# The opening of a two-layer hybrid diffusion block: first modulation by column chunks, squares added on the vector engine

## The chip, the cores and the metric

The kernel runs on one core of one Trainium2 chip. It is written engine by engine: TensorE (PE) for matrix products, VectorE (DVE), ScalarE (ACT) and GpSimd (POOL) for the rest, SyncE (SP) for issuing transfers. Each engine works through its own list in order, and semaphores tie the lists together. The metric is device time of one execution in microseconds (us), the median over runs; all arithmetic is float32.

## The reference

Two layers over 256 latent tokens and 256 context tokens of width 1024. What matters here is the start of a layer:

```
ml = (silu(c) @ w_mod[l] + b_mod[l])            # 6 x 1024 numbers for the latent tokens
mc = (silu(c_ctx) @ w_mod[l] + b_mod[l])        # the same for the context tokens
hl = rms_norm(xl, norm1_g) * (1 + ml[1]) + ml[0]
hc = rms_norm(xc, norm1_g) * (1 + mc[1]) + mc[0]
pl, pc = hl @ w_in[l], hc @ w_in[l]             # combined input projection, then three token mixers
```

One of the mixers (Hyena) needs filter spectra that depend on weights alone: a small two-layer sine network (`fw1`, `fw2`, angle and sine each time), a third product `w3s` times a decay (the filters), its absolute sum, and a discrete Fourier transform of the sum and the difference of its two halves. Each layer has two such filters, o = 0 and o = 1. After the mixers come an output projection, a second modulated norm and a mixture of 16 experts.

## The kernel before

Activations stand feature-major: `xT` is 128 partitions x 8 blocks x 512 tokens. Before a projection the modulated input is split into a leading and a trailing part, `h_hi` and `h_lo` (block k of 8), and each weight half (128 columns) into `w_hi` and `w_lo`; a tile of the projection is 8 k-steps of three matmuls (lines 1020 to 1022). The first two tiles of layer 0 are run abreast, k-step by k-step (`proj_steps`), so that they can begin when block 0 of the input is ready; tiles 2, 3, ... follow whole.

All weights of the opening pass through a ring of 3 slots of 1 MB. The Python list `order` says what goes through it and in which order; SP issues the loads in that order, each behind a wait for its slot. In the kernel before the list starts with the 8 pieces of the first modulation (`("mod", 0, k)`: 128 rows of `w_mod`, columns 0 to 2047), then the chunks of `w_in` (`("in", 0, i)`), two weight halves each. The slot of a `w_in` chunk is free once GpSimd has written `w_lo` of both its halves (`trail`), which follows ScalarE's `w_hi` (`lead_in`).

The opening of layer 0, by engine:

- TensorE: the sums of squares for the norm as 8 matmuls with a matrix of ones (`norm_sum`), the 8 modulation pieces (`mod`, each adds its 128 rows to the same bank), the filter products (`filters(0, 0)`), `spectra_a`, transposes of the modulation row (`mod_columns`), `spectra_b`, `filters(0, 1)`, then the two tiles abreast. Tile 3 waits until DVE has finished tiles 0 and 1 (`pe.wait_ge(j_d[l], g - 1)`).
- ScalarE: squares of `xT`, two sines, the rough inverse root of the norm, copies of spectra and of the modulation row, `lead_in`, then the latent half's scale and shift and `h_hi`, block by block.
- VectorE: angles of the sines, the norm's mean and refinement (`norm_dve_root`), `taps` (filter products times decay, sum, difference, absolute values), the modulation's bias and gain, then for each block the norm's scale (line 2241), the context half's scale and shift (line 2246) and `h_lo` (line 2254), three blocks behind; after that `taps(0, 1)` and the short convolution of each tile (lines 2366 and 2368).

## Time and profile before

| | us |
|---|---|
| median of 3 runs (lowest, highest) | 1566.31 (1566.29, 1572.91) |
| the profiled execution's own time | 1569.26 |
| its span in the trace | 1567.6 |
| TensorE busy in the span | 1471.8 (94%) |
| first k-step of the two tiles abreast starts | 54.68 |

The profiled execution took 2.95 us more than the median, and 1.66 us of its time lie outside the span. In the rows below a time is counted from the start of the span. A group of matmuls in a timeline counts each float32 matmul as two records.

### The profile page before, as it was taken

The page shows a single profiled execution, that of the slowest core. Times are in us where ns is not written, and L with a number is a line of the kernel's source. Part 1 is how long each engine was busy: PE and PEld are TensorE (multiplying, and loading weights), DVE is VectorE, ACT ScalarE, POOL GpSimd, SP SyncE. Part 2 cuts the span into 40 slices and gives each one's busy share as a digit, 9 for nine tenths or more (in the row PEclk, how much of TensorE's full clock was granted, in tenths as well). Part 3 has the DMA queues.
Part 4 walks back from the last instruction along what each step waited for, and adds up shares of the span by engine and source line. Part 5 has one row for each costly group of instructions (what it writes and reads, how often), then busy time and mean ns, then how long its engine had stood idle before and what let it go on. Part 6 is the DMA issues. An engine that isn't in the chain of part 4 may idle for free.

```text
span 1567.6 us, 20695 instructions
## 1 busy us (share of the span) xinstructions
PE 1471.8 (94%) x8212; PEld 1086.9 (69%) x8212; DVE 877.5 (56%) x1266; ACT 632.7 (40%) x853; POOL 406.1 (26%) x367
## 2 busy tenths in 40 slices
PE   6999999899999997899999999999988997999997
PEld 2588788657777784678888874697868995445444
DVE  4725556774222347799999967664783566111112
ACT  2532222264222335477787755442264443010102
POOL 0446334201333440111101013473414661000000
PEclk9999999999999998899999999998999999999997
DMA  8423211376456573799999983252304766899993
GB/s 330 147 81 107 81 55 59 133 279 223 160 191 205 190 277 126 267 370 403 406 409 405 397 314 122 65 185 81 102 22 152 259 233 276 329 420 420 422 421 133
DMA packets 116898, 362.78 MB, mean 231 GB/s; under 512 B 7774, under 2 KB 73632, under 8 KB 85952
## 3 DMA queue, kind: packets, MB, share of 16 engines
q1 hardware_dynamic: 109296, 334.62, 56.5%
q0 software_dynamic: 7504, 26.81, 4.6%
q8 instruction: 67, 1.10, 0.3%
q14 instruction: 31, 0.25, 0.0%
HBM read 349.86 MB, written 11.53 MB: 231 GB/s over the span
## 4 chain that ended last, share of the span: by engine, by line
PE 49%; DVE 10%; issue 2%; ACT 1%; DMA 0%; POOL 0%; DVEq 0%; PEldq 0%; ACTq 0%
PE bank L1020 9%; PE bank L1021 9%; PE bank L1022 9%; PE bank L1540 7%; PE bank L1579 4%; PE bank L1493 2%; PE bank L1479 1%; PE bank L1549 1%; PE bank L1504 1%; PE bank L1097 1%; PE bank L1231 1%; PE bank L1606 1%; PE bank L1011 1%; PE bank L1607 1%; DVE mix L2403 0%
## 5 line engine op out<-in xcount | busy, mean ns | idle before, releaser
L833 POOL TENSOR_TENSOR w_lo<-ring,w_hi 128x256 fp32r<-128x256 f32 (+1 forms) x300 | 347.8, 1188 | 515.0 <-ACT w_hi L1864 515.0
L1020 PE MATMUL bank<-h_hi,w_hi 128*128 128x512 f32 (+1 forms) x768 | 272.1, 354 | 8.8 <-POOL w_lo L833 3.4
L1021 PE MATMUL bank<-h_hi,w_lo 128*128 128x512 f32 (+1 forms) x768 | 263.1, 343 | 0.0
L1022 PE MATMUL bank<-h_lo,w_hi 128*128 128x512 f32 (+1 forms) x768 | 263.0, 342 | 0.0
L1020 PEld LDWEIGHTS bank<-h_hi,w_hi 128*128 128x128 f32 x768 | 146.5, 191 | 41.1 <-issue 16.5
L1021 PEld LDWEIGHTS bank<-h_hi,w_lo 128*128 128x128 f32 x768 | 146.6, 191 | 16.8 <-issue 1.4
L1022 PEld LDWEIGHTS bank<-h_lo,w_hi 128*128 128x128 f32 x768 | 146.5, 191 | 16.8
L1020 PE MATMUL bank<-w_hi,h_hi 128*128 128x512 f32 (+1 forms) x384 | 141.8, 369 | 6.7 <-DVE h_lo L2785 3.1
L1864 ACT ACTIVATE w_hi<-ring 128x1024 fp32r<-128x1024 f32 x120 | 125.4, 1052 | 40.5 <-PE bank L1020 31.4
L1021 PE MATMUL bank<-w_hi,h_lo 128*128 128x512 f32 (+1 forms) x384 | 138.1, 360 | 0.0
L1022 PE MATMUL bank<-w_lo,h_hi 128*128 128x512 f32 (+1 forms) x384 | 137.7, 359 | 0.0
L2561 DVE SCALAR_TENSOR_TENSOR mix<-mix,bank 128x512 f32<-128x512 f32 (+1 forms) x48 | 26.5, 553 | 168.5 <-PE bank L1022 116.7
L1020 PEld LDWEIGHTS bank<-w_hi,h_hi 128*128 128x128 f32 x384 | 74.1, 193 | 17.7 <-issue 3.7
L2043 ACT ACTIVATE mix<-bank 128x256 f32<-128x256 f32 (+1 forms) x39 | 18.8, 481 | 165.9 <-PE bank L1022 164.2
L2617 DVE TENSOR_TENSOR w_lo<-ring,w_hi 128x2048 fp32r<-128x2048 f32 x32 | 73.3, 2292 | 17.4 <-ACT w_hi L2073 17.4
L1022 PEld LDWEIGHTS bank<-w_lo,h_hi 128*128 128x128 f32 x384 | 74.0, 193 | 10.8
L1021 PEld LDWEIGHTS bank<-w_hi,h_lo 128*128 128x128 f32 x384 | 74.1, 193 | 10.4 <-issue 0.5
L2617 DVE TENSOR_TENSOR w_lo<-mix,w_hi 128x2048 fp32r<-128x2048 f32 x32 | 73.1, 2284 | 2.3 <-ACT w_hi L2073 2.3
L2073 ACT ACTIVATE w_hi<-mix 128x2048 fp32r<-128x2048 f32 x32 | 61.4, 1918 | 22.1 <-PE bank L1022 22.1
L994 POOL TENSOR_SCALAR mix<-xT,fin_g 128x256 f32<-128x256 f32 x4 | 3.6, 919 | 253.8 <-DVE xT L2917 253.8
L2073 ACT ACTIVATE w_hi<-ring 128x2048 fp32r<-128x2048 f32 x32 | 61.2, 1915 | 19.3 <-PE bank L1022 19.3
L1540 PE MATMUL bank<-operands_plain,mix 128*64 128x512 f32 x248 | 63.9, 594 | 0.0
(367 smaller groups left out, 2865.6 us busy)
## 6 DMA issues: line engine op xcount, KB each, us to landing
ring<-in_w_in SPq DMA_DIRECT2D x52, 1024.0 KB, 5.0
mix<-in_w_gate_e SPq DMA_DIRECT2D x40, 1024.0 KB, 7.8
ring<-in_w_up_e SPq DMA_DIRECT2D x38, 1024.0 KB, 8.1
mix<-in_w_down_e SPq DMA_DIRECT2D x25, 1024.0 KB, 8.3
ring<-in_w_mod SPq DMA_DIRECT2D x24, 1024.0 KB, 6.0
ring<-in_w_down_e SPq DMA_DIRECT2D x23, 1024.0 KB, 7.5
mix<-in_w_mod SPq DMA_DIRECT2D x19, 1024.0 KB, 4.9
operands_plain<-in_w_up_e SPq DMA_DIRECT2D x16, 1024.0 KB, 12.3
```

Source lines behind the costliest of these rows:

```text
L833: last = pool.tensor_tensor(w_lo[:, slot, k:k + n], rview(raw, 8)[:, k:k + n, x * P:(x + 1) * P], w_hi[:, slot, k:k + n].bitcast(F32), ALU ...
L1020: first = mm(dst, stat[0], mov[0], start=start, stop=False)
L1021: mm(dst, stat[1], mov[0], start=False, stop=False)
L1022: return first, mm(dst, stat[0], mov[1], start=False, stop=stop)
L1493: last = mm(bank[i][:, k * P:(k + 1) * P], htok[:, j, (4 * i + k) * P:(4 * i + k + 1) * P], hot_rows[l][e % 2][:, j, :], start=j == 0, sto ...
L1540: last = mm(dst[x * M:(x + 1) * M, :], heT[:, 0, 4 * h + k, x * M:(x + 1) * M], raw(l, c)[:, k * FF:(k + 1) * FF], start=h + k == 0, stop= ...
L1579: last = mm(y_bank[o][x * M:(x + 1) * M, :], hidT[:, 0, 2 * h + k, x * M:(x + 1) * M], raw(l, c)[:, k * D + o * 512:k * D + (o + 1) * 512] ...
L1864: A(w_hi[:, slot], rview(raw, 8)[:, :, x * P:(x + 1) * P], ACT.Copy).then_inc(w_h, 1)
L2043: A(gate_t[:, m % 2, 0:T], gate_v, ACT.Tanh, scale=0.5).then_inc(g_t[l], 1)
L2073: A(xhi[c % XH], raw(0, c), ACT.Copy).then_inc(x_wh, 1)
L2561: last = V.scalar_tensor_tensor(gated, gate_t[:, m % 2, 0:T], 1.0, bank[2 + m % 2][:, 0:T], ALU.add, ALU.mult)
L2617: V.tensor_tensor(xlo[c % XH], raw(0, c), xhi[c % XH].bitcast(F32), ALU.subtract).then_inc(x_wd, 1)
```

## The change

- `w_mod` of the first modulation is laid out on the host in 8 column chunks (`w_mod_first`): piece p holds, for all 1024 input rows, the 128 shift columns and the 128 gain columns of feature block p. A piece therefore gives the finished modulation of block p alone (`first_piece`: 8 matmuls of 32 rows x 256 columns; four strips of the bank hold partial sums). ScalarE copies the strips (`first_rows`), TensorE adds the strips and turns them into columns with `strip_sum` (`first_columns`), and DVE adds the bias and makes the gain (`first_take`) for blocks 0 to 3 together, 4, 5, 6, and 7. ScalarE scales block k when its part is there (`first_scale`).
- The first `w_in` chunk moves in the ring order to behind the first four modulation pieces.
- `w3s` and `decay` are loaded ahead of the modulation pieces.
- The 8 squares are added on DVE (`squares_added`, 7 additions) and one matmul sums the result, in place of 8 matmuls.
- DVE puts the norm's mean between the two parts of `taps(0, 0)`, and its refinement before the absolute values.
- `spectra_a`, `spectra_b` and the first k-steps of the tiles abreast are cut into steps and set between the pieces; `filters(0, 1)` moves behind the two tiles abreast.

```diff
+IN_AFTER = 4
+MORE = 7
+TAKES = [(0, 4), (4, 5), (5, 6), (6, 7), (7, 8)]
+TAKES_AT = [0, 2, 4, 5, 7]
...
         order = [("mod", 0, k) for k in range(DK)]
+        order.insert(IN_AFTER, ("in", 0, 0))
...
+            def first_piece(p):
+
+                at = at_of[("mod", 0, p)]
+                pe.wait_ge(ring_full[at % RS], full_at(at))
+                if p:
+                    pe.wait_ge(m_ev[0], p)
+                for j in range(2):
+                    for c in range(4):
+                        k = 2 * c + j
+                        last = mm(bank[5][32 * c:32 * c + 32, 0:256], csil[:, k, :], ring[:, at % RS, k * 256:(k + 1) * 256],
+                                  start=j == 0, stop=j == 1)
+                last.then_inc(ring_used, 1)
+
+            def first_columns(p):
+
+                pe.wait_ge(m_ev[0], p + 1)
+                if p >= TAKES[0][1]:
+                    pe.wait_ge(m_tk[0], p)
+                for c in range(2):
+                    last = mm(bank[6][:, 4 * p + 2 * c:4 * p + 2 * c + 2], piece_rows[p % 2][:, c * P:(c + 1) * P], strip_sum,
+                              start=True, stop=True)
+                last.then_inc(m_co[0], 1)
 
             filter_in(0, 0)
+            filter_in(0, 1)
             pe.wait_ge(s_ld, 16 * 2)
-            for k in range(4):
-                norm_sum(0, NT, k)
             pe.wait_ge(s_c, 2)
-            mod(0, 0, 0)
-            filter_in(0, 1)
-            for k in range(4, DK):
-                norm_sum(0, NT, k)
-            mods_and_filters(0, range(1, DK))
-            filters(0, 1)
+            filters(0, 0)
+            first_piece(0)
+            norm_sum_added(0, NT)
+            first_piece(1)
...
-                for _ in zip(*(proj_steps(g) for g in range(ABREAST[l]))):
+                abreast_steps = zip(*(proj_steps(g) for g in range(ABREAST[l])))
+                if l == 0:
+                    a_steps, b_steps = spectra_a_steps(0, 0), spectra_b_steps(0, 0)
+                    first_columns(0)
+                    first_piece(2)
+                    first_columns(1)
+                    next(a_steps)
+                    first_piece(3)
+                    first_columns(2)
+                    next(a_steps)
+                    first_piece(4)
+                    first_columns(3)
+                    next(b_steps)
+                    first_piece(5)
+                    first_columns(4)
+                    next(b_steps)
+                    next(abreast_steps)
+                    first_piece(6)
+                    first_columns(5)
+                    next(b_steps)
+                    next(abreast_steps)
+                    first_piece(7)
+                    first_columns(6)
+                    next(abreast_steps)
+                    first_columns(7)
+                for _ in abreast_steps:
                     pass
+                if l == 0:
+                    filters(0, 1)
...
+                    first_rows(1)
+                    first_rows(2)
+                    first_rows(3)
+                    lead_in(0)
+                    lead_in(1)
+                    spectrum_a(0, 0)
+                    first_rows(4)
+                    first_scale(0)
...
+            def first_take(lo, hi):
+
+                n = hi - lo
+                dve.wait_ge(m_co[0], hi)
...
+                        if inst == 0 and k in TAKES_AT:
+                            first_take(*TAKES[TAKES_AT.index(k)])
...
             angle(0, 0)
             angle(0, 1)
-            norm_dve_root(0, NT)
-            taps(0, 0)
-            mod_first(0)
+            dve.wait_ge(s_ld, 16 * 2)
+            V.tensor_reduce(strip_sum, ident.rearrange("p (c x) -> p x c", c=4)[:, 0:2], AX.X, ALU.add)
+            for k in range(1, DK):
+                squares_added(0, NT, k)
+            taps(0, 0, norm_dve_mean)
+            norm_dve_rest(0, NT)
+            taps_size(0, 0)
```

How it moves the lists, at three places. The first is SP's list at its start (`in_w_mod` and `in_w_mod_first` are modulation pieces, `in_hy_w` is `w3s`, `in_w_in` a chunk of the projection). Before:

```order
L711 DMA xT<-in_x_cols 128x4096
L779 DMA ring<-in_w_mod 128x2048 x3
L715 DMA mix<-in_hy_w 128x1024
L716 DMA mix<-in_decay 128x1024
L718 DMA dft_f<-in_dft_f 128x1024
L719 DMA nyq<-in_nyq 128x2
L779 DMA ring<-in_w_mod 128x2048 x5
L779 DMA ring<-in_w_in 128x8x256
```

and of the change:

```order
L725 DMA xT<-in_x_cols 128x4096
L726 DMA mix<-in_hy_w 128x1024
L727 DMA mix<-in_decay 128x1024
L798 DMA ring<-in_w_mod_first 128x2048 x3
L735 DMA dft_f<-in_dft_f 128x1024
L736 DMA nyq<-in_nyq 128x2
L798 DMA ring<-in_w_mod_first 128x2048
L798 DMA ring<-in_w_in 128x8x256
L798 DMA ring<-in_w_mod_first 128x2048 x4
L744 DMA dft_z<-in_dft_z 128x512
```

The projection chunk now stands ahead of four of the modulation pieces, and the filter weights ahead of all.

The second place is TensorE's list from the filter products to the end of the first half of `spectra_b` (L1070 and L1092 filters, L1047 and L1151 modulation pieces, L1079 and L1108 `spectra_a`, L1161 `first_columns`). Before:

```order
L1070 MATMUL bank<-mix 128x512 x4
L1047 MATMUL bank<-ring,csil 32x512 x8
L1079 MATMUL bank<-mix,dft_f 128x512 x4
L1082 MATMUL bank<-mix,nyq 1x512 x2
L1047 MATMUL bank<-ring,csil 32x512 x8
L1029 MATMUL bank<-square,mix 128x128 x4
L1092 MATMUL bank<-square,mix 128x1 x8
```

and of the change:

```order
L1161 MATMUL bank<-small,mix 128x2 x2
L1108 MATMUL bank<-mix,dft_f 128x512 x2
L1113 MATMUL bank<-mix,nyq 1x512 x2
L1151 MATMUL bank<-ring,csil 32x256 x8
L1161 MATMUL bank<-small,mix 128x2 x2
L1129 MATMUL bank<-square,mix 128x1 x8
L1151 MATMUL bank<-ring,csil 32x256 x8
```

Each piece is now followed by its own small column products, and by a part of the spectra.

The third place is TensorE's list where the two tiles abreast end. Before, the second filter (L1070) stands ahead of them:

```order
L1092 MATMUL bank<-square,mix 128x1 x8
L1097 MATMUL bank<-mix,dft_f 128x512 x4
L1070 MATMUL bank<-mix 128x512 x4
L1020 MATMUL bank<-h_hi,w_hi 128x512
L1021 MATMUL bank<-h_hi,w_lo 128x512
L1022 MATMUL bank<-h_lo,w_hi 128x512
```

and of the change, where it (L1092) stands between the last k-step of tiles 0 and 1 and the first of tile 2:

```order
L1039 MATMUL bank<-h_hi,w_hi 128x512
L1040 MATMUL bank<-h_hi,w_lo 128x512
L1041 MATMUL bank<-h_lo,w_hi 128x512
L1092 MATMUL bank<-mix 128x512 x4
L1039 MATMUL bank<-h_hi,w_hi 128x512
```

`filters(0, 1)` has moved from ahead of 16 k-steps to behind them.

## Rows read from the trace of the kernel before

**Rows 1.** The page's first line.

```profile
span 1567.6 us, 20695 instructions
```

**Rows 2.** Timeline of TensorE, 50 to 78 us: start, duration, line, operation.

```profile
52.45 1.99 PE L1070 MATMUL bank<-mix 64*128 64x512 f32 x8 [1.72 <-ACT mix L1838]
54.68 0.47 PE L1020 MATMUL bank<-h_hi,w_hi 128*128 128x512 f32 x1 [0.24 <-DVE h_lo L2254]
...
71.70 3.60 PE L1079 MATMUL bank<-mix,dft_f 128*128 128x512 f32 x8
75.23 1.88 PE L1082 MATMUL bank<-mix,nyq 128*1 128x512 f32 x4
77.03 0.50 PE L1020 MATMUL bank<-h_hi,w_hi 128*128 128x512 f32 x1
```

**Rows 3.** Timeline of VectorE, second filter and first convolutions.

```profile
63.59 2.48 DVE L2310 TENSOR_TENSOR mix<-bank,mix 128x512 f32<-128x512 f32 x4
...
75.15 0.75 DVE L2368 SCALAR_TENSOR_TENSOR mix<-bank,par,mix 128x510 f32<-128x510 f32 x1
```

**Rows 4.** Timeline of TensorE, 12 to 52 us.

```profile
12.50 6.68 PE L1004 MATMUL bank<-mix,square 128*128 128x512 f32 x8 [6.78 <-ACT mix L1772]
19.10 1.07 PE L1047 MATMUL bank<-ring,csil 128*32 128x512 f32 x8
...
30.43 1.06 PE L1047 MATMUL bank<-ring,csil 128*32 128x512 f32 x8 [1.25 <-DMA ring<-in_w_mod]
32.93 1.94 PE L1047 MATMUL bank<-ring,csil 128*32 128x512 f32 x8 [1.43 <-DMA ring<-in_w_mod]
...
45.34 1.84 PE L1092 MATMUL bank<-square,mix 128*128 128x1 f32 x16
47.05 3.68 PE L1097 MATMUL bank<-mix,dft_f 128*128 128x512 f32 x8
```

**Rows 5.** Busy time by stretch: engines, granted clock, DMA share, GB/s.

```profile
core 0: us, PE busy (x) PEld busy (x) DVE busy (x) ACT busy (x) POOL busy (x), PEclk, DMA share, GB/s
...
30.00:32.00 2.00, 1.06 (x8) 0.16 (x8) 1.84 (x4) 0.00 (x0) 0.00 (x0) 1.00 1.01 426
32.00:34.00 2.00, 1.07 (x8) 0.20 (x8) 1.97 (x3) 0.00 (x0) 0.00 (x0) 0.55 1.02 430
...
38.00:40.00 2.00, 2.00 (x5) 0.72 (x3) 0.00 (x0) 0.00 (x0) 0.00 (x0) 0.74 0.85 274
```

**Rows 6.** Timeline of ScalarE, 11 to 47 us.

```profile
11.72 1.15 ACT L1772 ACTIVATE mix<-xT 128x512 f32<-128x512 f32 x2 [6.93 <-DMA xT<-in_x_cols]
...
44.69 2.00 ACT L1864 ACTIVATE w_hi<-ring 128x1024 fp32r<-128x1024 f32 x2
```

**Rows 7.** Timeline of VectorE, 20 to 56 us.

```profile
20.84 0.54 DVE L2293 TENSOR_SCALAR mix<-bank,par 128x256 f32<-128x256 f32 x1 [12.19 <-PE bank L1058]
...
23.45 0.29 DVE L2301 TENSOR_SCALAR mix<-mix 128x256 f32<-128x256 f32 x1
...
29.29 2.48 DVE L2310 TENSOR_TENSOR mix<-bank,mix 128x512 f32<-128x512 f32 x4 [0.99 <-PE bank L1070]
...
36.11 1.23 DVE L2321 TENSOR_TENSOR mix<-mix 128x1024 f32<-128x1024 f32 x1
...
45.77 0.80 DVE L2274 SCALAR_TENSOR_TENSOR gs<-mods,par 128x8 f32<-128x8 f32 x2
46.49 1.81 DVE L2241 TENSOR_TENSOR mix<-xT,mix 128x512 f32<-128x512 f32 x2
...
53.84 0.69 DVE L2254 TENSOR_TENSOR h_lo<-mix,h_hi 128x512 fp32r<-128x512 f32 x1 [1.07 <-ACT h_hi L1805]
...
55.05 0.41 DVE L2246 TENSOR_SCALAR mix<-mix,gs,mods 128x256 f32<-128x256 f32 x1
```

**Rows 8.** Timeline of GpSimd, the trailing halves of the weights.

```profile
45.82 7.53 POOL L833 TENSOR_TENSOR w_lo<-ring,w_hi 128x256 fp32r<-128x256 f32 x8 [45.25 <-ACT w_hi L1864]
62.72 2.85 POOL L833 TENSOR_TENSOR w_lo<-ring,w_hi 128x256 fp32r<-128x256 f32 x4 [9.37 <-ACT w_hi L1864]
```

**Rows 9.** SP's queue, modulation pieces 4 to 6 being issued.

```profile
25.61 2.05 SPq L779 DMA_DIRECT2D ring<-in_w_mod x3
```

More of the change, by code:

```diff
@@ L231, in build @@
         mod_next = area(16384, 2048)
+        piece_rows = [area(21504 + 256 * i, 256) for i in range(2)]
+        strip_sum = small[:, 12:14]
         mrows = [[area(o, 512) for o in (21504, 17536, 19968)], [area(o, 512) for o in (19968, 19968)]]
@@ L1065, in filters @@
                     pe.wait_ge(f_a[l], 6 * l + 2)
-                    pe.wait_ge(s_lds, transforms_to(l))
+                    if l:
+                        pe.wait_ge(s_lds, transforms_to(l))
+                    else:
+                        pe.wait_ge(s_ldl[0], 32)
                 for j in range(2):
@@ L1083, in spectra_a, with spectra_b_steps @@
                 last.then_inc(f_p[l], 1)
+                yield
             def spectra_b(l, o):
+                for _ in spectra_b_steps(l, o):
+                    pass
+            def spectra_b_steps(l, o):
                 pe.wait_ge(f_d[l], 10 * l + 5 + 4 * o)
@@ L1788, in norm_act_scale @@
                     if w == 0:
[L1789 to L1791 removed]
+                        scale_h(inst, k)
                         if k:
@@ L1884, in _ @@
                     act.wait_ge(j_pe[l], g + 1)
+                    if l == 0 and g == 0:
+                        act.wait_ge(f_p[l], 6)
                     if g in (4, 8):
@@ L2301, in angle, with taps @@
                 V.tensor_scalar(x0, x1, 3.1415925, -3.1415925, ALU.min, ALU.max).then_inc(f_d[l], 1)
-            def taps(l, o):
+            def taps(l, o, between=None):
                 r, pm = fraw[l][o], fpm[l][o]
                 dve.wait_ge(f_p[l], 8 * l + 3 + 3 * o)
-                dve.wait_ge(s_lds, transforms_to(l))
+                if l:
+                    dve.wait_ge(s_lds, transforms_to(l))
+                else:
+                    dve.wait_ge(s_ldl[0], 32)
                 for i in range(2):
@@ L2313, in taps @@
                 dve.wait_ge(dve_c, chain[0])
+                if between is not None:
+                    between(2 * l, NT)
                 link(V.memset(r[0:1, 1, 0, :], 0.0))
@@ L2317, in taps, with taps_size @@
                 V.tensor_tensor(pm[:, 1], r[:, 0], r[:, 1], ALU.subtract).then_inc(f_d[l], 1)
+                if between is None:
+                    taps_size(l, o)
+            def taps_size(l, o):
+                r = fraw[l][o]
                 dve.wait_ge(f_d[l], 10 * l + 4 + 4 * o)
```

144 lines of the change are left out of this document (92 added, 52 removed).

## The prediction

> **What bounds the kernel now.** I read the page first for the span, 1567.6 us [rows 1], then the timelines of the five engines over the first 110 us, since nothing else is rebuilt. TensorE has three stages there. Up to 54.68 it waits often: for `xT`, then for modulation pieces (idle 1.25 and 1.43 us ahead of two of them), then for a ScalarE copy, and at 54.68 for the first `h_lo` [rows 2, 4]. From there it runs without a gap: tiles 0, 1 and 2 are 72 matmuls from 54.68 to 71.70, that is 5.67 us a tile and 1.42 us for a k-step of two tiles abreast; then `spectra_a(0, 1)` (3.60 and 1.88), then tile 3 at 77.03 [rows 2]. So whatever the change does to the time is what it does to the start of tile 3, which I use as the mark: from 77.03 on both kernels have the same lists on each engine, and the loads behind it are released by engines that stand later in the same chain, so they move with it.
>
> One more reading matters. In the trace before, VectorE starts `taps(0, 1)` at 63.59, as soon as it is through with `h_lo`, because the products of `filters(0, 1)` have been ready since 54.44. It has done the convolutions of tiles 0 and 1 at 75.90 [rows 3]: 12.3 us of work. Tile 3 needs them. In the kernel before they are 1.1 us early, so the wait is not seen.
>
> **The change, step by step.** I write hops between engines as 0.1 us.
>
> *Up to VectorE's first block.* `xT` lands at 11.7 [rows 6]. The second filter layer's angle takes 2.9 (20.84 to 23.74 [rows 7]). Its matmul is now ahead of it: one of 128x512 took 1.67 (6.68 for four [rows 4]), this one has half the columns; with the sine of about 0.4 the angle runs 13.2 to 16.2. An addition of squares is one of the 0.69 operations [rows 7]; the first ends at 17.1, squares 2 and 3 (0.6 each [rows 6]) stand ahead of the second sine on ScalarE, so that ends at 18.8. The seven additions end near 22.4.
>
> *TensorE's clock here.* The four matmuls from 12.50 took 1.67 us each, while at full clock four of the same size took 3.60 [rows 2, 4]: the engine starts at the lower of its two levels (1.2 GHz), though no clock event shows it. The row for 32 to 34 us shows it granted 0.55 after two gaps around a single piece, and the piece from 32.93 took 1.94 in place of 1.06; it came back at 39, with the engine busy all the while [rows 4, 5]. In the changed kernel TensorE has nearly nothing to do before 18.8, so I take `filters(0, 0)` at the lower level: 2 x 1.99 less the tail, 3.8 [rows 2], to 22.6; piece 0 1.94, to 24.6; the norm's matmul 0.9 to 1.7 [rows 2, 4], to 25.8; piece 1 to 26.9.
>
> *VectorE.* Before, `taps(0, 0)` is 8.05 from 29.29 to 37.34 [rows 7]. Its first 2.5 are done at 25.2, the mean (0.7) at 26.5, then 5.6 for the rest and 2.1 for three refinements: 34.2. It starts block 0 there and not at 46.49 [rows 7]. That is 12.3 us earlier, and it is the most the change can hand on.
>
> *The ring.* Piece 1 frees the slot of the `w_in` chunk, issued at 27.0. A load into an idle queue was issued at 25.61 and used at 30.43, 4.8 us [rows 4, 9], so it lands at 31.9. ScalarE copies the rows of pieces 1 to 3 first; piece 3 stands behind half of `spectra_a` (1.8) and ends at 32.0. Then the two `w_hi` (2.0 [rows 6]), the first done at 33.4, and GpSimd's eight operations: 7.53 beside a busy VectorE, 2 x 2.85 = 5.7 with a less busy one [rows 8]. VectorE waits part of that time for its columns, so I take the middle, 6.6: done at 40.1. SP's next load, piece 6, waits for exactly this, and piece 7 and all tables stand behind it in SP's list. Piece 6 lands at 40.2 + 4.8 = 45.0, piece 7 one transfer later: 1 MB at 426 GB/s [rows 5] is 2.5, so 47.5.
>
> The Trainium skill (SBUF — State Buffer, "SBUF: two separate sides") states that VectorE and GpSimd share a port pair under an exclusive lock, taken by whichever starts first, when a VectorE operation has two SBUF inputs. By that, GpSimd would stretch to the 7.53 only while VectorE is working, and pieces 6 and 7 would come up to 0.9 us later or earlier than I take it; the trace agrees in kind, with 7.53 for eight operations beside VectorE's busiest stretch.
>
> *The tiles abreast.* Piece 4 follows the second half of `spectra_a` (2.8, with the two row products) and ends at 36.1, so blocks 0 to 3 have their modulation near 37. Piece 5 follows the sums of `spectra_b` (1.84 [rows 4]) and ends at 39.2, its columns at 39.5. VectorE must take block 4 before it reaches `h_lo` of block 0: take 0.6, context scale 0.4, norm scale 0.7, context scale 0.4, `h_lo` 0.7 [rows 7] put k-step 0 at 42.3 instead of 54.68. But VectorE's list puts the take of block 5 ahead of `h_lo` 1, of block 6 ahead of `h_lo` 2, of block 7 ahead of `h_lo` 4. After piece 6 (45.1 to 46.1, columns 0.3) come a take (about 0.6: one operation of 0.40 and a smaller one), the context scale (0.41) and `h_lo` (0.69) [rows 7]: k-step 1 at 48.2 to 49.6, piece 7 to 50.7, again 2.1 on the chain: k-step 2 at 52.8 to 54.3, k-step 3 at 54.6 to 56.1; a further 2.4 of VectorE's list (scale, take, context, `h_lo`) puts k-step 4 at 57.2, and the last ends at 62.9. Before, tiles 0 and 1 ended at 54.68 + 11.3 = 66.0. So of the 12.3 us, 3.1 are left here.
>
> *Behind them.* `filters(0, 1)`, 1.99 [rows 2], now comes here and ends at 64.9. From there TensorE needs tile 2 and `spectra_a`, 5.67 + 5.33 = 11.0, but VectorE needs 12.3 from the same moment, and tile 3 waits for VectorE: 64.9 + 0.1 + 12.3 = 77.3. That is 0.3 us later than before. The 1.1 us of slack are used, and the wait for the columns and the second filter's late start have eaten the rest.
>
> *The clock once more.* Between 40.2 and 45.1 TensorE has 1.4 us of work. The gaps that lost the clock before were shorter [rows 4, 5], so I expect the lower level at about 44. Piece 6 then costs 0.9 more, and the second half of `spectra_b` behind it (half of 3.68 [rows 4]) about 1.8 more, of which some is hidden behind the chain over VectorE. With recovery somewhere in there, this is 0.9 to 2.9; I take 1.7. The Trainium skill (TensorE: Matmul & The Clock Gate, "What's actually happening") says that the throttled state is the default and that activity releases it. That rule speaks against a list with a wait between every two pieces; by the rows the same comes out.
>
> Sum: +0.3 + 1.7 = +2.0 us. Against its own execution that is 1569.26 + 2.0 = 1571.3; that execution stood 2.95 above the median of 1566.31, so the median is forecast at 1568.3. Removed work (7 matmuls of the norm, the transposes) stands at nothing, since TensorE waits there anyway; if that cover were gone it would be 7 x 0.9 = 6 us.
>
> **Rivals.**
>
> 1. *The clock stays up, GpSimd runs free.* Pieces 6 and 7 come 0.9 earlier and no matmul is slow: 77.3 - 0.9 = 76.4, 0.6 us before 77.03, and a load latency shorter than 4.8 adds to it. 1564.5 to 1566.5. For it: VectorE idles beside GpSimd; against it: the gap at 40 to 45. Chance 0.25.
> 2. *The early start is kept.* If `w_lo` is done much sooner, k-steps run back to back from 42.3: 11.4 for the steps, 2.1 for two pieces, 1.8 for `spectra_b`, 0.9 for columns, 2.0 for the filter: 60.5, mark at 72.9, gain 4.1: 1562.2. Against it stands piece 6's release by GpSimd; it needs `w_lo` at 35, before ScalarE's second `w_hi`. Chance 0.07. More than 4.8 I can't make out of the rows, so faster by over 0.5% would need something outside the opening.
> 3. *The low clock spreads* (other side). If TensorE is at the lower level from 24 to 32 too, pieces 1 to 3 and half of `spectra_a` cost 4.5 more, all ahead of the ring's chain; piece 6 lands near 49 and the mark is at 81 to 83: +4 to +6, 1570.5 to 1572.5. Chance 0.2. It decides for slower once the level also lasts over tile 2 and `spectra_a`, 11.0 us more: then +8 to +14, 1574 to 1580, chance 0.06.
> 4. *It doesn't arrive:* a shift at tile 3 is absorbed later. The later stages have nothing fixed in time that I can see; chance 0.02, 1566.3.
>
> **How the numbers follow.** My case (1566.6 to 1570.5) has 0.4, the rivals 0.25, 0.07, 0.2, 0.06 and 0.02. For 8 in 10 the range goes from 1564.0 to 1573.0. About 0.5% (7.8 us) is what a measurement of this kernel tells from no change; nearly all cases are inside: faster 0.03, same 0.90, slower 0.07.
>
> **What would show it.** In the changed kernel's timeline: VectorE's first block scale near 34, k-step 0 near 42, then gaps of TensorE ahead of pieces 6 and 7 with SP waiting for GpSimd's `w_lo`; granted clock at 0.5 somewhere from 40 to 50; `filters(0, 1)` ending near 65 to 67; tile 3 waiting 1.3 us for VectorE's convolution, starting near 79. Wrong would be: k-steps without gaps from 42 (then rival 2), a clock of 1.00 throughout (rival 1), or a change of duration in stages behind tile 3.

## The result

| us | kernel before | changed kernel |
|---|---|---|
| median of 10 runs each (lowest, highest) | 1566.9 (1564.33, 1572.97) | 1575.34 (1570.36, 1580.17) |
| ratio, 95% interval | | 1.0047 (1.0034 to 1.0060) |
| profiled execution: own time, span | 1569.26, 1567.6 | 1574.6, 1572.9 |
| tile 3 starts | 77.03 | 79.14 |

The changed kernel is slower by 7.4 us by the ratio, 5.3 to 9.4 by its interval (the medians differ by 8.4). The forecast was 1568.3 with a range from 1564.0 to 1573.0.

The page of the changed kernel begins so; it answers to [rows 1], and its third line counts TensorE's records (8212 of each sort before):

```profile
span 1572.9 us, 20920 instructions
## 1 busy us (share of the span) xinstructions
PE 1469.7 (93%) x8290; PEld 1088.3 (69%) x8290; DVE 876.7 (56%) x1281; ACT 635.1 (40%) x861; POOL 403.7 (26%) x367
```

TensorE's timeline of the changed kernel from 39 to 80 us, beside [rows 2, 4]. L1151 is a modulation piece, L1161 its columns, L1135 the halves of `spectra_b`, L1039 the first matmul of a k-step, L1092 `filters(0, 1)`:

```profile
39.91 1.07 PE L1151 MATMUL bank<-ring,csil 128*32 128x256 f32 x16
...
41.79 3.76 PE L1135 MATMUL bank<-mix,dft_f 128*128 128x512 f32 x4
44.56 1.42 PE L1039 MATMUL bank<-h_hi,w_hi 128*128 128x512 f32 x1
...
47.92 1.07 PE L1151 MATMUL bank<-ring,csil 128*32 128x256 f32 x16
...
49.38 1.96 PE L1135 MATMUL bank<-mix,dft_f 128*128 128x512 f32 x4
...
52.67 1.07 PE L1151 MATMUL bank<-ring,csil 128*32 128x256 f32 x16
...
55.66 0.50 PE L1039 MATMUL bank<-h_hi,w_hi 128*128 128x512 f32 x1 [1.38 <-DVE h_lo L2389]
...
64.72 1.99 PE L1092 MATMUL bank<-mix 64*128 64x512 f32 x8
...
79.14 0.50 PE L1039 MATMUL bank<-h_hi,w_hi 128*128 128x512 f32 x1 [1.53 <-DVE mix L2528]
```

The same half of `spectra_b` takes 3.76 us at 41.79 and 1.96 at 49.38: the lower clock, which the busy times by stretch give for 40 to 48 us:

```profile
36.00:40.00 4.00, 3.41 (x40) 2.81 (x44) 1.59 (x3) 1.93 (x4) 3.61 (x6) 1.00 0.35 147
40.00:44.00 4.00, 4.00 (x23) 2.36 (x24) 3.08 (x9) 2.40 (x5) 0.00 (x0) 0.61 0.82 293
44.00:48.00 4.00, 4.00 (x12) 2.08 (x14) 0.79 (x2) 0.00 (x0) 0.00 (x0) 0.54 1.00 378
```

Two rows of VectorE, one of GpSimd and one of SP's queue, in this order, show the chain that was forecast: block 0 is scaled at 33.56, the trailing halves end at 39.6 and not at 53.3 [rows 8], and SP issues its last two modulation pieces (6 and 7) when they end. VectorE waits 5.12 us for the second filter's products ("issue": no releaser shown; the products of 64.72 end as it starts).

```profile
33.56 0.68 DVE L2372 TENSOR_TENSOR mix<-xT,mix 128x512 f32<-128x512 f32 x1
...
66.81 2.48 DVE L2446 TENSOR_TENSOR mix<-bank,mix 128x512 f32<-128x512 f32 x4 [5.12 <-issue]
```

```profile
33.85 5.77 POOL L852 TENSOR_TENSOR w_lo<-ring,w_hi 128x256 fp32r<-128x256 f32 x8 [33.27 <-ACT w_hi L1955]
```

```profile
28.34 12.10 SPq L798 DMA_DIRECT2D ring<-in_w_mod_first  x4
```

One link of that chain isn't there. TensorE never waits for these two loads. Piece 6 is issued at 39.64, and by the DMA rows of 39.5 to 39.9 us it lands 4.8 us later, at 44.4:

```profile
ring<-in_w_mod_first SPq DMA_DIRECT2D x1, 1024.0 KB, 4.8
```

TensorE starts piece 6 only at 47.92 and piece 7, landed at 47.0, at 52.67; neither row has idle time before it, and the engine is busy for 4.00 of 4.00 us in both stretches from 40 to 48. What holds piece 6 is TensorE's own list: half of `spectra_b` and k-step 0 at the lower clock stand ahead of it. From piece 6 to piece 7 it is then 4.75 us, a round over the engines: columns, VectorE's take, context scale and `h_lo`, k-step 1, next piece.

Tile 3 is 2.1 us later than in [rows 2], as forecast, but the span is 5.3 us longer. One place far behind shows where more went. At the end of layer 1 TensorE takes a branch (an overflow of an expert's tokens, which doesn't happen here) and adds the last expert's rows. First the changed kernel, then the kernel before:

```profile
1556.09 0.38 PE L1683 MATMUL bank<-mix_parts 128*128 128x256 f32 x1 [4.07 <-issue]
```

```profile
1549.76 0.38 PE L1606 MATMUL bank<-mix_parts 128*128 128x256 f32 x1 [2.35 <-DVE mix_parts L2812]
```

Before, TensorE is released by VectorE; after, by nothing that the trace names, 1.7 us later.

### The profile page after: what moved, and what is told of

Same layout as the page of the kernel before. It is cut to its first block, busy times and chain, and to the rows that moved or that the text cites. A ratio compares the mean times of both kernels' runs of the same rounds, so it can differ in the third digit from the quotient of the medians.

```text
span 1572.9 us, 20920 instructions
## 1 busy us (share of the span) xinstructions
PE 1469.7 (93%) x8290; PEld 1088.3 (69%) x8290; DVE 876.7 (56%) x1281; ACT 635.1 (40%) x861; POOL 403.7 (26%) x367
## 3 DMA queue, kind: packets, MB, share of 16 engines
q8 instruction: 68, 1.11, 0.3%
## 4 chain that ended last, share of the span: by engine, by line
PE 45%; DVE 10%; issue 3%; ACT 1%; POOL 1%; DMA 1%; SPq 0%; DVEq 0%; PEldq 0%; POOLq 0%; ACTq 0%
PE bank L1039 8%; PE bank L1041 8%; PE bank L1040 8%; PE bank L1617 7%; PE bank L1656 4%; PE bank L1570 2%; POOL w_lo L852 1%; PE bank L1556 1%; PE bank L1626 1%; PE bank L1581 1%; DMA ring<-in_w_branch 1%; PE bank L1135 1%; PE bank L1308 1%; PE bank L1030 1%; DVE mix L2563 0%
## 5 line engine op out<-in xcount | busy, mean ns | idle before, releaser
L1039 PE MATMUL bank<-h_hi,w_hi 128*128 128x512 f32 (+1 forms) x768 | 274.2, 357 | 12.5 <-DVE h_lo L2389 3.4
L1039 PEld LDWEIGHTS bank<-h_hi,w_hi 128*128 128x128 f32 x768 | 146.9, 191 | 45.7 <-issue 16.0
L1039 PE MATMUL bank<-w_hi,h_hi 128*128 128x512 f32 (+1 forms) x384 | 140.8, 367 | 6.7 <-DVE h_lo L2932 3.1
L1039 PEld LDWEIGHTS bank<-w_hi,h_hi 128*128 128x128 f32 x384 | 73.6, 192 | 17.6 <-issue 3.7
```

The lines of the kernel that those rows point to most:

```text
L1039: first = mm(dst, stat[0], mov[0], start=start, stop=False)
```

## The experiments

Each kernel was timed against the kernel before on the same chip; ratios are to it. "Tile 3" is the start of that tile in the run's profile, comparable with 77.03 and 79.14.

### Is it the layout of the data, and does the order in the ring matter?

`a_again` is the changed kernel once more, to see whether the loss is scatter. `a_last` declares `w_mod_first` behind all other arrays (the same line, 15 lines further down). `b_own` is the kernel before, whose first pieces are read from an array of their own, declared at that place:

```diff
+    data["w_mod_first"] = np.ascontiguousarray(np.asarray(w_mod)[0, :, 0:2 * D]).reshape(DK, P, 2 * D)
...
+                        if i < DK:
+                            src = a["w_mod_first"][i]
```

`a_in5`:

```diff
-IN_AFTER = 4
+IN_AFTER = 5
```

> The changed kernel once more, unaltered, as the yardstick for the runs beside it. Theory A (the loss behind tile 3 is scatter of later stages between single executions): tile 3 again starts near 79.1, but what is added between tile 3 and the end differs from the 3.2 us of the first profile, and the median here stands 2 to 5 us above the kernel before. Theory B (a real second loss behind tile 3): median 6 to 9 us above, and the same places of the trace are late again: the two pool and Hyena products near 300, the output of the mixers from 1205 to 1260.

> The host declares the array w_mod_first behind all other inputs, so that w_in, w_branch, w_out and the expert weights lie where they lie in the kernel before; the instructions are the same. Theory B1 (the 8 MB put in front of the weights shift their addresses, and transfers of the later stages come slower): 3 to 6 us faster than the changed kernel, near 1569. Theory A or any theory in which the loss is made on the engines: same as the changed kernel within 1.5 us.

> The kernel before, with the first modulation read from an array of its own (same rows, same order, 8 pieces of 1 MB) that is declared at the place of w_mod_first. Only addresses differ from the kernel before. Theory B1: 3 to 6 us slower than the kernel before. Otherwise: within 1.5 us of it.

> The first w_in chunk moves one place back in the ring order (IN_AFTER 5), so that only modulation piece 7, and no longer piece 6, waits for GpSimd's w_lo. Theory of the opening as forecast (the ring wait sets k-steps 1 to 4, and the clock falls in the gap it leaves): the gap of TensorE ahead of piece 6 shrinks from some 3 us to under 1.5, tile 3 starts 1.5 to 3 us earlier, near 77, and the time falls by as much. Rival (what binds is VectorE's take of the next block, whatever the ring does): tile 3 within 0.7 us of 79.1.

| run | median us | ratio (95%) | tile 3 | wait at the last branch |
|---|---|---|---|---|
| a_again | 1574.65 | 1.0048 (1.0035 to 1.0061) | 79.74 | 3.63 issue |
| a_last | 1573.71 | 1.0047 (1.0034 to 1.0060) | 77.83 | 3.63 issue |
| b_own | 1568.38 | 1.0013 (1.0000 to 1.0026) | 74.36 | 2.35 DVE |
| a_in5 | 1575.07 | 1.0045 (1.0032 to 1.0058) | 79.34 | 3.63 issue |

The loss is repeated by `a_again` (theory B) and isn't scatter. The place of the array changes nothing. `a_in5` failed as an idea, and its rival is right: tile 3 is within 0.7 us of 79.1. Piece 6 no longer waits for GpSimd and is loaded 2.8 us earlier (landed at 41.7 instead of 44.4), yet it starts at 48.13 and piece 7 at 52.88, as in the changed kernel (47.92 and 52.67). TensorE wasn't waiting for the load. From piece 6 to piece 7 it is 4.74 to 4.76 us in all twelve profiles of kernels with k-step 1 between them, whatever their clock and their loads.

`b_own` turned up a fault of the yardstick. Busy times by stretch, 20 to 40 us, first of the kernel before as in the profile that the prediction used, then of `b_own`; the last three numbers are granted clock, DMA share, GB/s:

```profile
20.00:40.00 20.00, 17.32 (x70) 5.54 (x66) 13.24 (x20) 3.59 (x5) 0.00 (x0) 0.83 0.89 336
```

```profile
20.00:40.00 20.00, 17.23 (x85) 5.29 (x85) 13.24 (x20) 3.98 (x7) 0.00 (x0) 1.00 0.87 345
```

The same work, but the profile of before had lost its clock for a while, and its tile 3 stood at 77.03 where `b_own` has 74.36. Four later profiles of kernels with this opening (`b_pad166`, `b_pad80`, `b_code42`, `b_code21`) have 1.00 in this stretch too. The yardstick had a loss in it of the kind that the forecast charged to the change.

### The clock

`a_early` puts three spare matmuls of 128x512 where TensorE idles before the first filter, `a_gap` three between 36 and 42 us; `b_busy` gives the kernel before one ahead of each of the two pieces that it waits for.

```diff
             pe.wait_ge(s_c, 2)
+            keep_busy(0, 3)
             filters(0, 0)
```

```diff
+                    keep_busy(0, 1)
                     first_piece(4)
                     first_columns(3)
+                    keep_busy(0, 1)
                     next(b_steps)
+                    keep_busy(0, 1)
```

```diff
                 for k in ks:
+                    if k in (3, 4):
+                        keep_busy(6, 1)
                     mod(l, 0, k)
```

> The changed kernel with three spare matmuls of 128x512 (the matrix of ones times the constants, into a bank that nobody reads before its first real matmul) ahead of the first filter products, where TensorE stands idle from 13.6 to 18.96 us in the profile of the changed kernel. If the lower starting level of TensorE's clock is what makes the filter products take 3.79 instead of 1.99 and piece 0 take 1.61 instead of 1.07, they take 2.0 and 1.07 here, and VectorE's list and the ring's first releases come 1.8 to 2.4 us earlier: tile 3 near 77 in place of 79.1, 1 to 2 us less. Rival: the opening is set by the loads and by GpSimd from piece 1 on, and the matmuls of the start only wait for something else; then tile 3 stays within 0.5 us of 79.1 although the filters get shorter.

> The changed kernel with one spare 128x512 matmul ahead of piece 4, one ahead of the column sums of the first spectrum and one behind them, 2.6 us of work at full clock, which keeps TensorE streaming from 36 to 42 us. If the clock falls to the lower level because of the thin activity between 35.8 and 41.8 (a gap, a piece, column products, column sums of one column each), the granted clock is near 1.00 from 40 to 48, the half of spectra_b there takes 2.0 instead of 3.76 and the first k-step 1.5 instead of 3.4, and piece 6 starts near 46.7 instead of 47.92: tile 3 1 to 2 us earlier, time down by as much. Rival: the clock falls anyway or its loss is hidden behind the load of piece 6; then the spare work is simply added, 0 to 1.5 us slower.

> The kernel before with one spare 128x512 matmul ahead of each of the two modulation pieces that TensorE waits for (1.25 and 1.43 us idle in its profile). If the gaps there are what loses the clock in some of its executions (tile 3 at 77.03 in the first profile, 75.2, 75.4 and 74.35 in three others), the granted clock is 1.00 from 20 to 60 and tile 3 stands at 74.4 to 75; the median comes down by the mean loss, 0.5 to 1 us. Rival: the spare matmuls delay the pieces as much as they save: no change of the median, tile 3 at 75 to 76.

| run | median us | ratio (95%) | tile 3 |
|---|---|---|---|
| a_early | 1572.76 | 1.0033 (1.0022 to 1.0045) | 78.96 |
| a_gap | 1574.02 | 1.0042 (1.0025 to 1.0060) | 78.55 |
| b_busy | 1568.75 | 1.0002 (0.9990 to 1.0015) | 73.98 |

In `a_early` the first filter took 1.99 us instead of 3.79, as expected, but tile 3 came only 0.2 earlier and not 2: the rival is right. TensorE was ahead of its suppliers then, idled 0.89 and 1.48 us at 22 and 25 us, and the clock fell behind these gaps as well; it fell again at 40 to 44 (0.70). `a_early`, busy times from 24 to 32 us:

```profile
24.00:28.00 4.00, 2.52 (x36) 1.52 (x26) 3.89 (x6) 1.27 (x3) 0.00 (x0) 0.99 0.97 358
28.00:32.00 4.00, 4.00 (x14) 1.48 (x17) 3.86 (x6) 0.02 (x1) 0.00 (x0) 0.58 0.99 328
```

In `a_gap` the clock held, 1.00 where the changed kernel has 0.61 and 0.54:

```profile
40.00:44.00 4.00, 4.00 (x32) 2.35 (x32) 1.45 (x5) 1.11 (x3) 0.00 (x0) 1.00 0.85 307
44.00:48.00 4.00, 3.41 (x22) 1.66 (x23) 2.23 (x5) 1.30 (x3) 0.00 (x0) 1.00 1.02 375
```

Piece 6 started at 47.33 instead of 47.92 (46.7 was expected) and tile 3 0.6 us earlier (1 to 2 expected): piece 5 stands behind the spare work and started at 41.76 instead of 39.91, and k-step 0 then waited 0.59 for `h_lo`. `b_busy` kept its clock, 1.00 from 20 to 60, and had tile 3 at 73.98 in its profile, but the same median: spare work at a wait is worth nothing that can be measured here.

Two later versions that execute no spare work, `a_code22` and `a_filt_code22` (below), kept the clock by themselves: 1.00 in every stretch of 4 us from 20 to 76. `a_code22`, where the changed kernel has 0.61 and 0.54:

```profile
40.00:44.00 4.00, 4.00 (x33) 2.44 (x33) 3.87 (x9) 2.55 (x6) 0.99 (x2) 1.00 0.50 152
44.00:48.00 4.00, 3.42 (x28) 1.97 (x27) 1.39 (x3) 0.82 (x3) 0.00 (x0) 1.00 0.98 401
```

It started 1.1 us late (`filters(0, 0)` at 20.02 against 18.96), and yet its tile 3 came 1.4 us earlier, at 77.71. So the low clock cost some 2.5 us in the changed kernel's profile, an estimate from one pair of profiles, and the opening is slower without it too: 77.71 beside 73.28 in `b_code21`, whose clock is 1.00 from 20 to 60.

### The second filter, and the chunk behind all pieces

`a_filt`, with ScalarE's `spectrum_b(0, 0)` moved from behind block 7 to behind `first_rows(7)`:

```diff
                     first_columns(7)
+                    filters(0, 1)
                 for _ in abreast_steps:
                     pass
-                if l == 0:
-                    filters(0, 1)
```

`a_in8` sets `IN_AFTER = 8`, runs pieces, columns and `filters(0, 1)` ahead of all k-steps on TensorE (the three `next(abreast_steps)` among the pieces go), and on ScalarE:

```diff
                     first_rows(3)
-                    lead_in(0)
-                    lead_in(1)
                     spectrum_a(0, 0)
...
                     first_rows(7)
+                    spectrum_b(0, 0)
+                    lead_in(0)
+                    lead_in(1)
```

> The changed kernel with the products of the second filter moved from behind the two tiles abreast to ahead of their k-steps 3 to 7, and ScalarE's copy of the second spectrum part (which they wait for) ahead of its blocks 4 to 7. In the changed kernel VectorE waits 5.12 us for these products and tile 3 waits 1.53 for VectorE. If the place of the products is that part of the loss, VectorE starts the second filter when it is through with the last trailing block, near 60, tile 3 waits for nothing and starts at 64.7 plus 2.0 less the gap of 1.4 that the products now fill, plus 11.0: near 77.5 in place of 79.1, 1.5 us less. Rival: the products delay the k-steps by their full 2.0 and ScalarE's copy holds up block 4; then tile 3 stays within 0.5 of 79.1.

> The changed kernel with the first chunk of the projection's weights back behind all eight modulation pieces, its leading halves behind the rows of piece 7 on ScalarE, the second filter's products and all column products ahead of the two tiles abreast, which then run without pieces between them. If what ate the early start is pieces 6 and 7 waiting for a slot that GpSimd's trailing halves free (done at 39.6 in the changed kernel), the pieces land one after the other until about 39, the chunk at about 41, the trailing halves end at 47 to 49, and from there 11.4 us of k-steps run without a gap to 59 to 61; tile 3 at 70 to 72.5, that is 7 us before the changed kernel and 3 before the kernel before: 1562 to 1565 if the loss behind the branch stays. Rival 1: the later chunk costs more than the waits, the k-steps start after 52 and tile 3 is at 75 or later, 1569 to 1573. Rival 2: TensorE stands idle ahead of the k-steps and runs them at the lower clock, 3 to 5 us less of the gain.

`a_filt`: 1574.05, ratio 1.0039 (1.0024 to 1.0054), tile 3 at 77.36 with no wait, 1.8 us earlier than 79.14. The place of the filter is that much in the profile and 1.3 us in the ratios, whose intervals overlap widely. `a_in8`: 1575.57, ratio 1.0053 (1.0035 to 1.0071), tile 3 at 81.61. My expectation of 70 to 72.5 was wrong by 9 us; rival 1 had tile 3 right, though the time is 2.6 us above its range. TensorE's timeline of `a_in8`:

```profile
49.09 0.58 PE L1161 MATMUL bank<-small,mix 128*128 128x2 f32 x4 [0.35 <-DVE mods L2339]
55.02 3.78 PE L1092 MATMUL bank<-mix 64*128 64x512 f32 x8 [5.34 <-DVE mods L2339]
58.73 0.79 PE L1039 MATMUL bank<-h_hi,w_hi 128*128 128x512 f32 x1
```

Pieces 6 and 7 were not on time either (43.65 and 47.14): they stand in TensorE's list behind `spectra_b` at the lower clock. The leading halves began only at 50, the filter waited for VectorE's take of block 7, which stands behind `h_lo` in VectorE's list, and the wait cost the clock once more (3.78 instead of 1.99). The run changes four things at once, so it doesn't tell what the place of the chunk alone is worth. Its premise, that pieces 6 and 7 wait for the slot, doesn't hold in the changed kernel's trace either.

### The wait at the last branch

TensorE's instructions are fetched while it runs: in every profile the trace counts 67 or 68 packets of 16 KB on one queue for instructions, 1.10 or 1.11 MB, and 16 KB are 256 instructions of 64 bytes. TensorE's compiled list has 17,416 machine instructions before and 17,584 after, as many as fill 68 to 69 such packets (156 of the 168 more are the 78 matmul and 78 weight-load records of the page). Transfers at the branch, in 40 slices of 0.3 us: the kernel before from 1540 us, the changed one from 1546:

```profile
GB/s 0 0 0 0 55 0 0 0 0 0 0 0 0 0 0 0 0 0 0 0 0 0 0 0 0 0 0 0 0 55 0 0 0 0 0 0 0 0 0 0
```

```profile
GB/s 0 0 0 0 0 0 0 0 0 0 0 0 0 0 0 0 0 0 0 0 0 0 0 0 0 55 0 0 0 0 0 0 0 0 0 0 55 0 0 0
```

Before, one packet lands 8.4 us ahead of the row sums of 1549.76 and one 1.0 ahead. After, none lands in the 10 us ahead of the branch; one lands 2.4 us ahead of the sums at 1556.09, 1.7 us after TensorE's last matmul ended, and one behind their start. That the late packet holds the branch's target is inferred from its time; the trace doesn't say what a packet holds. The Trainium skill (Runtime: NRT & Kernel Launch, "Instruction fetch mechanics") states that an engine's instructions are prefetched in sequence in blocks of 16 KiB, 256 instructions, and that a taken branch whose target isn't in the two blocks at hand must fetch it before the engine goes on. By that rule 168 more instructions anywhere ahead can turn a hidden fetch into a stall; the trace agrees, with the packet that comes 1.7 us after the last matmul and the 1.7 us of longer wait.

The first attempts to shift the list, 64 and 128 empty instructions in the changed kernel and 80 and 166 in the kernel before, shifted nothing: empty instructions take no room in TensorE's list (it has 17,416 or 17,584 as without them). They are repetitions, then, and show what the timing resolves.

> The changed kernel with 64 empty instructions at TensorE's start, where it waits for its first load until 4.72 us. They move all of its later instructions by 64 places and do nothing else. In four profiles of changed kernels TensorE waits 3.6 to 4.1 us for nothing that the trace shows before the last sums of expert rows, behind a branch; before the change it waited 2.35 us for VectorE there. If that is the fetching of instructions and depends on where the branch's target lies in the list, the wait changes here, down to the 2.35 of VectorE at best: 1.3 us less. Rival: it comes from something else than the position; then it stays at 3.6 to 4.1 and the time at that of the changed kernel within 0.7 us.

> The kernel before with 166 empty instructions at TensorE's start, as many as the change adds to TensorE's list (39 more float32 matmuls of four machine instructions each, and ten others). If the position of the branch's target is the cause of the longer wait before the last sums of expert rows, the wait appears in the kernel before too: 3.6 us of issue in place of 2.35 for VectorE, and the time is 1.3 us up, 1568.2 beside 1566.9. Rival: it stays at 2.35 and the time within 0.7 us of the kernel before.

> The changed kernel with 128 empty instructions at TensorE's start, as before with 64. The trace shows the fetching of instructions as packets of 16 KB on a queue of its own: one around the wait behind the last branch in three profiles of the kernel before, two in all of the changed ones, 64 places later too. If the wait comes from where the branch's target lies in these blocks, 128 places move it to another part, and the wait falls to VectorE's 2.35 with one packet: 1.3 us less. If it is not the place, 3.6 to 4.2 stays.

> The kernel before with 80 empty instructions at TensorE's start. 166 left the wait behind the last branch at 2.35. If a float32 matmul counts as one instruction in the fetched blocks, the changed kernel's list is 49 places later and not 166, and its bad range (49 to 113 by the two profiles) holds 80: the wait becomes 3.6 to 4.2 with two packets, 1.3 to 1.8 us more. If the place is not the cause, it stays at 2.35.

| run | median us | ratio (95%) | tile 3 | wait at the last branch |
|---|---|---|---|---|
| a_pad64 | 1575.64 | 1.0041 (1.0027 to 1.0055) | 78.30 | 4.17 issue |
| a_pad128 | 1573.79 | 1.0033 (1.0019 to 1.0048) | 78.38 | 3.99 issue |
| b_pad166 | 1567.58 | 0.9999 (0.9990 to 1.0008) | 75.38 | 2.35 DVE |
| b_pad80 | 1567.77 | 0.9998 (0.9987 to 1.0010) | 75.19 | 2.35 DVE |

What does take room are matmuls in the arm of layer 0's branch that no execution takes:

```diff
                     if l:
                         sum_rows(NS - 1)
+                    else:
+                        keep_busy(0, 22)
```

`a_code22` brings the changed kernel's list to 17,672 instructions, which leaves 8 over whole blocks as 17,416 does; `b_code42` brings that of before to 17,584 (176 over), `b_code21` to 17,500 (92 over).

> The changed kernel with 22 more matmuls written into the branch of layer 0 that no execution here takes (more tokens for an expert than its room). Nothing is executed besides, but TensorE's later instructions lie 88 machine instructions further, at the same place within the blocks of 16 KB in which the trace shows them fetched as in the kernel before. The empty instructions of the two pairs of runs before left every fetch of TensorE where it was, since they take no room in its list, so the place has not been tried yet. If the place is the cause, the wait ahead of the last sums of expert rows is VectorE's 2.35 again, with a block fetched 8.5 us ahead of it as before the change, and the kernel is 1.3 to 1.8 us faster than the changed one: 1573. Rival: the wait stays at 3.6 to 4.2 and has another cause.

> The kernel before with 42 more matmuls in that branch, 168 machine instructions, as many as the change adds to TensorE's list. If the place is the cause, the kernel before now has the wait of 3.6 to 4.2 in place of 2.35, no block fetched 8.5 us ahead, and is 1.3 to 1.8 us slower than the kernel before. Rival: 2.35 stays and so does the time.

> The kernel before with 21 matmuls in the branch that is not taken, 84 machine instructions: a third place between that of the kernel before and that of the changed one. If the loss comes where the last branch's target begins a block that has not been fetched yet, this place either has it in full (wait of 3.6, ratio 1.0017 or more) or not at all (2.35, ratio 1.000). Rival: it grows with the distance, then wait and ratio lie between.

| run | median us | ratio (95%) | tile 3 | wait at the last branch |
|---|---|---|---|---|
| a_code22 | 1570.13 | 1.0017 (1.0005 to 1.0030) | 77.71 | 2.35 DVE |
| b_code42 | 1571.81 | 1.0017 (1.0003 to 1.0031) | 74.97 | 3.61 issue |
| b_code21 | 1566.49 | 0.9991 (0.9977 to 1.0005) | 73.28 | 2.35 DVE |

From both sides the wait went with the place, here in `a_code22` and in `b_code42`:

```profile
1550.29 0.39 PE L1683 MATMUL bank<-mix_parts 128*128 128x256 f32 x1 [2.35 <-DVE mix_parts L2961]
```

```profile
1551.46 0.39 PE L1606 MATMUL bank<-mix_parts 128*128 128x256 f32 x1 [3.61 <-issue]
```

All 11 profiles with the list at the changed kernel's place (or 12 instructions behind it, `a_early` and `a_gap`) have 3.6 to 4.2 us there, with a packet 2.4 to 2.5 us ahead of the sums, and all nine others have 2.35 and no packet between 8.0 and 1.1 us ahead. From the start of tile 3 to the end it is 1491.9 to 1501.5 us in the 11 (median 1493.8) and 1488.3 to 1492.1 in the nine (median 1490.6): 3.2 us. (The 1501.5 is `a_gap`, whose profiled execution was 7.7 us above its median; the next is 1498.0.)

The timed effect is larger than the wait and than the 1.3 to 1.8 us that were expected of these two runs: 0.30% less in `a_code22` (4.7 us, from 1.0047; 2.5 us from `a_pad128`, the lowest repetition of the changed kernel) and 0.17% more in `b_code42` (2.7 us). Some of the rest is seen at the branch of layer 0, though not in every run (`b_code42` 2.07 us of issue at 958.9, and `b_code21` 1.91 without being slower). Some may be in the second layer between 1200 and 1327 us, where the 11 profiles at that place are longer than the first profile of before by about 2 us on average and the nine others by under 1 (the exact numbers depend on the matmuls between which one measures). That part wasn't settled.

### What is left, together

`a_filt_code22` is `a_filt` with the 22 matmuls; `a_all` has the three spare matmuls of `a_early`, the three of `a_gap`, `a_filt`'s edits and 16 matmuls in the arm.

> The changed kernel with the two edits that helped on their own and nothing spare executed: the second filter's products ahead of k-step 3 (1.3 to 1.8 us alone) and TensorE's later list back at the place in the fetched blocks that it had before the change (about 4.5 alone). If both hold, the median is at 1568.3 to 1569 and the ratio to the kernel before 1.000 to 1.001: then place and filter are what the change lost, and the early start and the waits cancel, as the prediction had it for the opening. Rival: the ratio stays at 1.0017 or above, and the opening itself keeps a loss of 2.5 us or more.

> The changed kernel with what helped one by one: the second filter's products ahead of k-step 3, three spare matmuls at the start and three between 36 and 42 us that hold the clock, and the list moved as in the run with 22 more matmuls (16 here, since the spare ones count). If the parts add up, 1.8 for the filter, 0.6 for the clock in the middle, 0.2 for the start and 1.5 for the place: tile 3 near 76.5 and a median near 1570.5, still 2 to 3 us above the kernel before, whose tile 3 is at 74.4 to 75.4 where its clock holds. Rival: they overlap, and the sum is 2 us or less; or the clock holds everywhere and tile 3 comes at 75, then the median is within 1 us of the kernel before.

`a_filt_code22`: 1570.68, ratio 1.0014 (1.0002 to 1.0026), above the 1.000 to 1.001 that was expected. Place and filter explain most of the loss, not all: 2.2 us stay (0.3 to 4.1), and beside `a_code22` the filter's place is worth 0.5 us, within the error. Its profile was of its fastest execution and has the clock at 1.00 throughout and tile 3 at 75.05. Only there does piece 6 wait for its load, and only 0.36 us. `a_all`: 1572.48, ratio 1.0025 (1.0008 to 1.0042), no better than its parts and above the 1570.5 that was expected. Its runs lie between 1567.55 and 1578.64. In its profile, one of the long ones, the clock fell three times, and tile 3 stood at 84.59. Its busy times by stretch, the granted clock third from the right:

```profile
28.00:32.00 4.00, 4.00 (x15) 2.03 (x8) 3.86 (x6) 0.38 (x1) 0.00 (x0) 0.50 0.88 290
44.00:48.00 4.00, 4.00 (x23) 1.32 (x23) 0.00 (x0) 0.57 (x2) 0.00 (x0) 0.57 0.99 405
...
64.00:68.00 4.00, 4.00 (x11) 1.94 (x8) 3.90 (x10) 1.37 (x2) 2.55 (x4) 0.51 0.00 0
```

No version beats the kernel before by more than the measurement tells; `b_code21` is the lowest median of the study, and its interval holds 1.

## Why the prediction was wrong, point by point

**The opening: right at its end, and partly by luck.** VectorE's block 0 was forecast for 34.2 and came at 33.56; piece 6's release by `w_lo` for 40.1, and came at 39.6; the low clock from 44 on came at 41; `filters(0, 1)` was to end at 65 to 67 and ended at 66.7; tile 3 was to wait 1.3 us for VectorE near 79 and waited 1.53 until 79.14. K-step 0 was 2.3 us later than 42.3, mostly since the clock fell before it and not behind it (43.30 in `a_filt_code22`, where it stayed up). GpSimd's eight operations took 5.77 us beside the 5.7 to 7.53 between which 6.6 was taken; they began 0.3 later than forecast, so the release came out right.

But the forecast had "gaps of TensorE ahead of pieces 6 and 7", with the load of piece 6 as what holds the chain ("Piece 6 lands at 40.2 + 4.8 = 45.0"). It landed at 44.4 and nobody waited for it: piece 6 started at 47.92, 2.8 us later than forecast, behind TensorE's own slow list. Each piece was then followed by its round over VectorE, as forecast (4.5 us by the forecast, 4.75 measured). The 2.8 shrank to 1.8 by the end of `filters(0, 1)`, 66.7 beside 64.9, and this is the 1.7 that the forecast had added for the clock. So the sum is right, while the wait that it names for pieces 6 and 7 is not.

**The base of the sum: the first step that failed.** "That execution stood 2.95 above the median, so the median is forecast at 1568.3" takes the excess of the profiled execution for something outside the comparison. It lay inside: from 20 to 40 us that execution had a granted clock of 0.83 where others had 1.00. Five profiles with the opening of the kernel before have tile 3 at 77.03, 75.38, 75.19, 74.97 and 73.28, 75.2 on average; six with that of the changed kernel have 79.14, 79.74, 77.83, 78.30, 78.38 and 77.71, 78.5 on average. The forecast tile 3 at 79.0 was right within 0.5 us of the six; against the typical 75.2 it is +3.8 and not +2.0, and the opening measured so is +3.3. That is 1.3 us of the miss. Of the 2.95, 1.9 lie ahead of tile 3 (77.03 against 75.2); from there on that execution took 1490.6 us, the median of its group of nine.

**"From 77.03 on both kernels have the same lists": the second step that failed, and the larger.** What comes behind tile 3 stood at nothing in the sum. The lists are the same, but they lie elsewhere: 168 instructions further, which is 3.2 us between the profiles and 2.5 to 4.7 by the timed runs on both sides. I had no rival for that. The measured time lies where rival 3 has its last case (1574 to 1580), but that case wants the low clock over tile 2 and `spectra_a`, and the granted clock is 1.00 from 48 to 76 us: the number would have been right by luck. I named "a change of duration in stages behind tile 3" as what would prove me wrong, and it did.

**The clock term** of 1.7 was of the right kind: in `a_gap` a clock of 1.00 gave 0.6 us of it back, net of 2.6 us of spare work, and `a_code22` shows some 2.5. What I did not see is that the term exists on both sides, and that it is a scatter as much as a cost. Rival 1 ("the clock stays up") put tile 3 at 76.4; with the clock up it came at 77.71.

**The filter behind the tiles** was charged by its chain (64.9 + 0.1 + 12.3); moving it gave 1.8 us in the profile, beside the 1.4 that this chain has over TensorE's 11.0.

The sum by the runs: place 2.5 to 4.7, filter 0.5 to 1.3, the rest of the opening about 2, together 5 to 8 for 7.4 measured. The place is shown from both sides; how the rest is shared between the clock and the rounds over VectorE stays open.

## What to carry to other kernels

Before adding a measured difference to a median, look whether the profile that you compare with is typical in the very stretch that the change touches; here four more profiles of the same opening had tile 3 1.7 to 3.8 us earlier. A kernel with branches has a cost that no row of work shows: count how many instructions a change adds ahead of a branch, and if a wait without a releaser appears behind it, shift the list (with instructions in an arm that is never taken) before judging the change. And before naming a load as what holds a chain, compare when it landed with when it was used: here 1 MB had been there for 3.5 us, and an experiment that had it there 2.8 us earlier still (`a_in5`) gained nothing.

## What the runs showed of the hardware

- 168 more instructions in an arm that is never taken, nothing else changed, cost 0.17% (0.03 to 0.31) of 1568 us (`b_code42`); behind the last branch a 16 KB packet landed 2.4 us ahead of the next matmul, after the last one had ended, where before it landed 8.4 us ahead. 84 more cost nothing that was measured (`b_code21`, 0.9977 to 1.0005).
- Empty instructions on TensorE take no room in its compiled list (17,416 or 17,584 with and without them); four kernels with 64 to 166 of them could not be told from those without.
- Speeding up an engine at the start can lose the clock later: with three spare matmuls and `filters(0, 0)` at 1.99 instead of 3.79 us, the granted clock fell to 0.58 from 28 to 32 us in `a_early` and to 0.50 in `a_all`; it was 1.00 there in the changed kernel.
